# Dense feed-forward up products: the activations' high and low parts side by side in one 512-column product

## The reference

```
def swiglu(x, w13, w2):                      # block 1, layer 0
    a, g = jnp.split(x @ w13, 2, axis=-1)
    return (jax.nn.silu(a) * g) @ w2

# block 2, each layer
h = rms_norm(x, norm_ffn_g[l])
u = causal_depthwise_conv(h @ ffn_w_up[l], ffn_conv_w[l], ffn_conv_b[l])   # width 3
x = x + (jax.nn.silu(u[..., :D_FF]) * u[..., D_FF:]) @ ffn_w_down[l]
```

## Time and profile before

| what | us |
|---|---|
| median of 3 runs (lowest, highest) | 2723.18 (2722.4, 2725.64) |
| the profiled execution, first to last instruction | 2724.5 |
| TensorE busy in it | 2412.8 (89%) |
| VectorE busy | 1805.8 (66%) |
| ScalarE busy | 1325.7 (49%) |
| GpSimd busy | 251.4 (9%) |

### The profile page before, as it was taken

The page is one execution under the profiler, slowest core; times in us unless marked ns, Lnnn a source line. Parts: engine busy times, 40 slices in busy tenths (PEclk is TensorE's granted clock), DMA queues, the critical chain, the costliest instruction groups (busy, mean ns, idle before and its releaser), DMA issues.

```text
span 2724.5 us, 42692 instructions
## 1 busy us (share of the span) xinstructions
PE 2412.8 (89%) x16461; PEld 2211.7 (81%) x16461; DVE 1805.8 (66%) x1724; ACT 1325.7 (49%) x1183; POOL 251.4 (9%) x208
## 2 busy tenths in 40 slices
PE   7879799777859999999999999997877998977998
PEld 7768799777859797979797979796766998866997
DVE  4454544546448687878787878787663677763776
ACT  3433333343327576767676767674342444332443
POOL 1300000130000000000000000000660000750000
PEclk9889899888969999999999999999877999967999
DMA  9224455522429798989898989897322455312451
GB/s 291 78 86 147 139 185 185 157 78 93 152 68 366 271 364 275 364 281 365 279 367 279 362 283 367 278 367 256 120 76 70 145 183 181 122 62 70 155 185 62
DMA packets 429765, 559.49 MB, mean 205 GB/s; under 512 B 9598, under 2 KB 384868, under 8 KB 429424
## 3 DMA queue, kind: packets, MB, share of 16 engines
q1 hardware_dynamic: 425376, 545.05, 59.2%
q0 software_dynamic: 4304, 13.25, 1.7%
HBM read 557.20 MB, written 1.06 MB: 205 GB/s over the span
## 4 chain that ended last, share of the span: by engine, by line
issue 44%; PE 39%; POOL 5%; DVE 5%; POOLq 3%; ACT 2%; DVEq 1%; DMA 1%; SPq 0%; ACTq 0%
PE ps L567 11%; PE ps L568 11%; PE ps L569 11%; POOL st L548 2%; POOLq L547 2%; POOL st L542 2%; POOL ht L491 1%; PE ps L600 1%; PE ps L1074 1%; PE ps L778 1%; PE ps L1054 1%; POOLq L495 1%; PE ps L752 0%; DVE xn L1505 0%; DVE w_lo L1443 0%
## 5 line engine op out<-in xcount | busy, mean ns | idle before, releaser
L1443 DVE TENSOR_TENSOR w_lo<-raw,w_hi 128x2048 fp32r<-128x2048 f32 x519 | 1191.3, 2302 | 448.9 <-ACT w_hi L1131 446.3
L1131 ACT ACTIVATE w_hi<-raw 128x2048 fp32r<-128x2048 f32 x519 | 985.4, 1908 | 245.1 <-PE ps L569 234.5
L567 PE MATMUL ps<-w_hi,xg_hi 128*128 128x256 f32 x1792 | 511.9, 286 | 16.3 <-DVE w_lo L1443 16.1
L568 PE MATMUL ps<-w_lo,xg_hi 128*128 128x256 f32 x1792 | 500.7, 279 | 0.0
L569 PE MATMUL ps<-w_hi,xg_lo 128*128 128x256 f32 x1792 | 500.7, 279 | 0.0
L567 PE MATMUL ps<-xT_hi,w_hi 128*128 128x256 f32 x1504 | 436.3, 290 | 22.7 <-DVE xT_lo L1458 15.0
L568 PE MATMUL ps<-xT_lo,w_hi 128*128 128x256 f32 x1504 | 433.1, 288 | 0.0
L569 PE MATMUL ps<-xT_hi,w_lo 128*128 128x256 f32 x1504 | 432.9, 288 | 0.0
L567 PEld LDWEIGHTS ps<-w_hi,xg_hi 128*128 128x128 f32 x1792 | 337.8, 188 | 26.7 <-DVE w_lo L1443 19.6
L568 PEld LDWEIGHTS ps<-w_lo,xg_hi 128*128 128x128 f32 x1792 | 341.5, 191 | 3.6
L569 PEld LDWEIGHTS ps<-w_hi,xg_lo 128*128 128x128 f32 x1792 | 337.9, 189 | 0.0
(11 more groups left out here) (458 smaller groups left out, 3150.0 us busy)
## 6 DMA issues: line engine op xcount, KB each, us to landing
raw<-in_exp_w SPq DMA_DIRECT2D x336, 1024.0 KB, 7.5
raw<-in_ffn_w_up SPq DMA_DIRECT2D x44, 1024.0 KB, 5.1
raw<-in_w_in SPq DMA_DIRECT2D x42, 1024.0 KB, 5.9
raw<-in_ffn_w SPq DMA_DIRECT2D x33, 1024.0 KB, 5.1
raw<-in_ffn_w_down SPq DMA_DIRECT2D x22, 1024.0 KB, 5.4
raw<-in_w_gate SPq DMA_DIRECT2D x16, 1024.0 KB, 5.3
raw<-in_w_out SPq DMA_DIRECT2D x8, 1024.0 KB, 5.0
raw<-in_w_o SPq DMA_DIRECT2D x6, 1024.0 KB, 5.0
```

Source lines behind the costliest of these rows:

```text
L567: pe.matmul(out, lhs[0], rhs[0], start=first, stop=False)
L568: pe.matmul(out, lhs[0], rhs[1], start=False, stop=False)
L1131: act.activation(w_hi[:, u.const % SPL, 0:width], raw[:, u.const % RAW, 0:width], ACT.Copy)\
L1443: dve.tensor_tensor(w_lo[:, u.const % SPL, 0:width], raw[:, u.const % RAW, 0:width], w_hi[:, u.const % SPL, 0:width].bitcast(F32), ALU.sub ...
```

## The change

`xT_hi` and `xT_lo` become two views of one tile `xT` in which, for each of the 8 chunks, the 256 columns of the high part lie beside the 256 of the low part. In the dense feed-forwards' up product the high weight block multiplies all 512 columns in one matmul, and the low weight block the 256 of the high part, into the first half of the same bank. The two halves of a bank are added afterwards: ScalarE copies the first halves out of PSUM, VectorE adds the second halves to the copy (`add_half`, one instruction of 2 x 256 elements and a drain). An up unit now needs two banks: A uses 4 and 5, G uses 6 and 7, in every step, and TensorE waits for the additions of the step before (`up_in`). In block 1 Silu is taken after the addition, from `sa` to `sa`, and `hf` first receives G. The counters of the two kinds of feed-forward become one set, so the counts of block 2 begin at DENSE_STEPS.

```diff
--- before.py
+++ after.py
@@ -197,8 +197,8 @@
         w_hi = sb("w_hi", [P, SPL, UW], F32R)
         w_lo = sb("w_lo", [P, SPL, UW], F32R)
         x = sb("x", [P, TT, D])
-        xT_hi = sb("xT_hi", [P, KC, S], F32R)
-        xT_lo = sb("xT_lo", [P, KC, S], F32R)
+        xT = sb("xT", [P, KC, 2, S], F32R)
+        xT_hi, xT_lo = xT[:, :, 0, :], xT[:, :, 1, :]
         yA_hi = sb("yA_hi", [P, 4, S], F32R)
         yA_lo = sb("yA_lo", [P, 4, S], F32R)
         with ExitStack() as shared:
@@ -340,8 +340,9 @@
         raw_landed = [ctx.enter_context(nc.semaphore(f"raw_landed{i}")) for i in range(RAW)]
         block = ctx.enter_context(nc.Block())
         yb, qgT, kgT, kdT, sTm = vb, qcT, laT, cumT, dm
-        F1 = {"h": hf, "h_ready": S_.h1_ready, "h_hi_ready": S_.h1_hi_ready, "h_lo_ready": S_.h1_lo_ready}
-        F2 = {"h": h2f, "h_ready": S_.h2_ready, "h_hi_ready": S_.h2_hi_ready, "h_lo_ready": S_.h2_lo_ready}
+        FF = {"half_ready": S_.half_ready, "up_in": S_.up_in, "h_ready": S_.h_ready, "h_hi_ready": S_.h_hi_ready,
+              "h_lo_ready": S_.h_lo_ready}
+        F1, F2 = {"h": hf, **FF}, {"h": h2f, **FF}
 
         def bank(b, *shape):
 
@@ -614,13 +615,22 @@
             def feed_forward(u, steps, count, hh, hl, sig):
 
                 def up(at, b):
-                    project_T(at, b)
+
+                    w = unit_parts(at, KC, FFC)
+                    for c in range(2):
+                        o = ps[:, b + c, :]
+                        for k in range(KC):
+                            hi, lo = [v[:, k, c * P:(c + 1) * P] for v in w]
+                            pe.matmul(o, hi, xT[:, k, :, :].rearrange("p a n -> p (a n)"), start=k == 0, stop=False)
+                            m = pe.matmul(o[:, 0:S], lo, xT_hi[:, k, :], start=False, stop=k == KC - 1)
+                    m.then_inc(S_.unit_used, 1)
 
                 def step_up(j, at, odd, dyn):
 
-                    pe.wait_ge(sig["h_ready"], dyn.value(plus=1))
-                    up(at, 4 + 2 * odd)
-                    up(at + 1, 5 + 2 * odd)
+                    pe.wait_ge(sig["up_in"], dyn.value(2, 1))
+                    up(at, 4)
+                    pe.wait_ge(sig["up_in"], dyn.value(2, 2))
+                    up(at + 1, 6)
 
                 def down(at, odd, dyn):
 
@@ -1118,7 +1128,7 @@
             with pe.Fori(0, 2) as L:
                 u = block2_units(passes).loop(L, LAYER2_UNITS)
                 mixer2(L, u)
-                feed_forward(u + MIX2_UNITS, DENSE_STEPS, Count(0).loop(L, DENSE_STEPS), h2_hi, h2_lo, F2)
+                feed_forward(u + MIX2_UNITS, DENSE_STEPS, Count(DENSE_STEPS).loop(L, DENSE_STEPS), h2_hi, h2_lo, F2)
                 close_sums()
 
 
@@ -1177,20 +1187,23 @@
 
             def silu1(at, odd, dyn, after):
 
-                act.wait_ge(S_.h1_ready, dyn.value(plus=1))
                 used(at)
-                act.activation(sa[:, odd], ps[:, 4 + 2 * odd, :], ACT.Silu).then_inc(S_.silu1_ready, 1)
+                act.activation(sa[:, odd].rearrange("p (c n) -> p c n", c=2), ps[:, 4:6, 0:S], ACT.Copy).then_inc(S_.half_ready, 1)
                 split(after)
+                act.wait_ge(S_.up_in, dyn.value(2, 3))
+                act.activation(sa[:, odd], sa[:, odd], ACT.Silu).then_inc(S_.silu1_ready, 1)
+                used(at + 1)
+                act.activation(hf[:, odd].rearrange("p (c n) -> p c n", c=2), ps[:, 6:8, 0:S], ACT.Copy).then_inc(S_.half_ready, 1)
 
             def conv2(at, odd, dyn, after):
 
-                act.wait_ge(S_.h2_ready, dyn.value(plus=1))
+                act.wait_ge(S_.h_ready, dyn.value(plus=1))
                 used(at)
-                act.activation(u_a[:, odd, :, 2:], bank(4 + 2 * odd, 2, S), ACT.Copy).then_inc(S_.ua_ready, 1)
+                act.activation(u_a[:, odd, :, 2:], ps[:, 4:6, 0:S], ACT.Copy).then_inc(S_.half_ready, 1)
                 split(after)
                 used(at + 1)
-                act.activation(u_g[:, odd, :, 2:], bank(5 + 2 * odd, 2, S), ACT.Copy).then_inc(S_.ug_ready, 1)
-                act.wait_ge(S_.ca_ready, dyn.value(plus=1))
+                act.activation(u_g[:, odd, :, 2:], ps[:, 6:8, 0:S], ACT.Copy).then_inc(S_.half_ready, 1)
+                act.wait_ge(S_.ca_ready, dyn.value(plus=1 - DENSE_STEPS))
                 act.activation(c_a[:, odd], c_a[:, odd], ACT.Silu).then_inc(S_.silu2_ready, 1)
 
             def mixer1(L, u):
@@ -1427,7 +1440,7 @@
                 u = block2_units(passes).loop(L, LAYER2_UNITS)
                 mixer2(L, u)
                 at = u + MIX2_UNITS
-                feed_forward(at, DENSE_STEPS, Count(0).loop(L, DENSE_STEPS), h2_hi, F2, conv2)
+                feed_forward(at, DENSE_STEPS, Count(DENSE_STEPS).loop(L, DENSE_STEPS), h2_hi, F2, conv2)
                 with act.If(L == 0):
                     split_next(at + STEP * DENSE_STEPS)
                 with act.Else():
@@ -1532,11 +1545,19 @@
                 for j in range(2 * pairs + 1, steps):
                     step(u + (2 + STEP * (j - 1)), j % 2, count + j, False)
 
+            def add_half(v, b):
+
+                dve.tensor_tensor(v, v, ps[:, b:b + 2, S:2 * S], ALU.add).then_inc(S_.up_in, 1)
+                dve.drain()
+
             def dense_hidden(at, odd, dyn, after):
+                dve.wait_ge(S_.half_ready, dyn.value(2, 1))
+                add_half(sa[:, odd].rearrange("p (c n) -> p c n", c=2), 4)
+                split(after)
+                dve.wait_ge(S_.half_ready, dyn.value(2, 2))
+                add_half(hf[:, odd].rearrange("p (c n) -> p c n", c=2), 6)
                 dve.wait_ge(S_.silu1_ready, dyn.value(plus=1))
-                split(after)
-                used(at + 1)
-                dve.tensor_tensor(hf[:, odd], sa[:, odd], ps[:, 5 + 2 * odd, :], ALU.mult).then_inc(S_.h1_ready, 1)
+                dve.tensor_tensor(hf[:, odd], sa[:, odd], hf[:, odd], ALU.mult).then_inc(S_.h_ready, 1)
 
             def less_max(sc, mx):
                 dve.reduce_max(mx, sc, AX_X)
@@ -2016,7 +2037,7 @@
             def conv_ffn(L):
                 def hidden(at, odd, dyn, after):
 
-                    j = Count(dyn.const, dyn.terms[1:]).value() * 2
+                    j = Count(dyn.const - DENSE_STEPS, dyn.terms[1:]).value() * 2
 
                     def columns(src, dst, first):
                         for k in range(3):
@@ -2032,20 +2053,22 @@
                                 dve.drain()
                         return m
 
-                    dve.wait_ge(S_.ua_ready, dyn.value(plus=1))
+                    dve.wait_ge(S_.half_ready, dyn.value(2, 1))
+                    add_half(u_a[:, odd, :, 2:], 4)
                     columns(u_a, c_a[:, odd], 0).then_inc(S_.ca_ready, 1)
                     split(after)
-                    dve.wait_ge(S_.ug_ready, dyn.value(plus=1))
+                    dve.wait_ge(S_.half_ready, dyn.value(2, 2))
+                    add_half(u_g[:, odd, :, 2:], 6)
                     columns(u_g, c_g, 22)
                     dve.drain()
-                    dve.wait_ge(S_.silu2_ready, dyn.value(plus=1))
+                    dve.wait_ge(S_.silu2_ready, dyn.value(plus=1 - DENSE_STEPS))
                     dve.tensor_tensor(h2f[:, odd].rearrange("p (c n) -> p c n", c=2), c_a[:, odd], c_g[:], ALU.mult)\
-                       .then_inc(S_.h2_ready, 1)
+                       .then_inc(S_.h_ready, 1)
                 return hidden
 
             dve.memset(zeros[:], 0.0)
-            dve.memset(stat[:, 1:2], 0.0).then_inc(S_.h1_ready, 2)
-            dve.memset(stat[:, 2:3], 0.0).then_inc(S_.h2_ready, 2)
+            dve.memset(stat[:, 1:2], 0.0).then_inc(S_.h_ready, 2)
+            dve.memset(stat[:, 2:3], 0.0).then_inc(S_.up_in, 2)
             dve.memset(stat[:, 3:4], 0.0).then_inc(S_.lo_ready, RAW)
             dve.memset(stat[:, 4:5], 0.0).then_inc(S_.xn_ready, 1)
             for n in range(AHEAD):
@@ -2068,7 +2091,7 @@
                 u = block2_units(passes).loop(L, LAYER2_UNITS)
                 mixer2(L, u)
                 at = u + MIX2_UNITS
-                feed_forward(at, DENSE_STEPS, Count(0).loop(L, DENSE_STEPS), h2_hi, h2_lo, F2, conv_ffn(L))
+                feed_forward(at, DENSE_STEPS, Count(DENSE_STEPS).loop(L, DENSE_STEPS), h2_hi, h2_lo, F2, conv_ffn(L))
                 with dve.If(L == 0):
                     split_next(at + STEP * DENSE_STEPS)
                 with dve.Else():
```

## The result

| kernel | median us (runs) | ratio to before, 95% interval |
|---|---|---|
| before | 2725.64 (7) | |
| changed | 2735.69 (7) | 1.0038 (1.0025 to 1.0051) |
| changed, run again later | 2736.14 (10), before 2726.93 (15) | 1.0035 (1.0022 to 1.0048) |

The changed kernel is 10 us slower. I had forecast 5.6 us slower, 2728.8, and a range up to 2734, so sign and place were right and the size was not. Part of the distance in absolute time isn't the change's: the median of the kernel before is 2725.64 over seven runs, where three had given 2723.18. The profiled execution of the changed kernel has a span of 2733.9 us, against 2724.5. The ratios of this document leave out two executions that took several times as long as all others, one of the kernel before (10206 us) and one of `best` (7705 us), and the medians count them.

The account below looks back on a forecast made before the run. TensorE was taken to bound both dense feed-forwards, with VectorE taking over block 2's step after the change. Block 1's -3.8 and block 2's +9.4 gave +5.6 us on the median 2723.18, so 2728.8 us, range 2724.5 to 2734.

Parts of the forecast that it names:

- TensorE in block 2: Block 2's dense feed-forwards: TensorE's own step falls from 17.10 to 16.70 us, as up units need fewer matmuls.
- VectorE's loop in block 2: Block 2's steps: 15.55 us without waits plus 1.91 for additions and lags gives 17.46, so VectorE sets the step, +0.36.
- PSUM banks and hand-shakes: Block 2's up units: giving up the second pair of PSUM banks costs nothing; additions free banks long before TensorE returns.
- Start of block 2: First steps of block 2's feed-forwards: G(1) begins 0.8 us later at the lower clock, c_g(1) is 1.4 late.
- End of block 2: Last down product, D(10), of block 2's feed-forwards: all lateness reaches the end, +4.7 us a layer, +9.4 for two.
- my high end: Upper forecast: block 1 saves 2.0 and loses 2.7 to the clock, block 2 +5.2 a layer; together +11, 2734 us.
- the loop that I closed on paper: Block 2's step timed from addition A at 0: nothing of TensorE's is late; it waits 0.7 us for G's weights.
- Block 1: Block 1's feed-forward: TensorE stays the bound; 19 up units save 0.20 each, 3.8 us (lower bound 2.0); start zero.
- (1): All three feed-forward stages: TensorE bounds them if additions cost VectorE under 1.15 us a step; 2713 us; chance 0.07.
- (2): Block 2's steps: TensorE's new small waits let its clock fall, some 20 falls cost 40 us; 2769; chance 0.06.
- (3): Block 2's steps: lag at the lower bound, 17.27 a step, little moves: +1.8, 2725; low end of forecast, no own chance.
- (4): Up product: halves don't run as one matmul, no 512-column rows on xT, TensorE slower; chance 0.02.

Follow-up runs that it names:

- best: Changed kernel plus block 2's first tap A on ScalarE, block 1's 512-column matmuls grouped first, 128-row fillers in block 2: 2715.87 us, 0.9951 of before.
- small_add: Changed kernel, but each block 2 addition covers only 2 of 256 columns of each bank: 2717.68 us, 0.9975 of before.
- tap_on_act: Changed kernel, but block 2's first tap over A runs on ScalarE instead of VectorE: 2721.13 us, 0.9985 of before.
- tap_order: tap_on_act, but each half of an up unit does its 8 matmuls of 512 columns before the 8 of 256: 2725.1 us (one run).
- double_add: Changed kernel with every addition done twice, the first into a spare tile, in both blocks: 2776.2 us (one run).
- tap_pad: tap_on_act with 24 bytes a partition left free ahead of block 2's tiles, aligning u, c and h to 1024 bytes: 2720.0 us (one run).
- before_fill: Kernel before with 14 matmuls of zeros between G(0) and A(1) of block 2's feed-forwards: 2724.24 us, 0.9996 of before.
- after_fill: Changed kernel with 32-row zero matmuls in block 2, 14 between G(0) and A(1), 12 before the last down product: 2736.06 us, 1.0033 of before.
- tap_on_act_fill: tap_on_act plus block 2 fillers, 14 between G(0) and A(1) and 5 before the last down product: 2715.89 us, 0.9966 of before.
- after_fill128: after_fill, but fillers have all 128 rows and move real xT against stationary zeros, 512 columns each: 2737.8 us (one run).

## Why the prediction was right and wrong

- **TensorE in block 2: right.** Its own step was forecast at 16.70 and measured 16.70 once VectorE was relieved (small_add, tap_on_act).
- **VectorE's loop in block 2: right.** Forecast 17.46, measured 17.50 and 17.55 in turn. Additions 0.68; the lags behind them 0.34 and 0.24 (forecast 0.31 and 0.22). The h2f product begins 0.16 to 0.20 behind the taps where it was 0.07, which I didn't have; its cause isn't shown.
- **PSUM banks and hand-shakes cost nothing: right** (small_add keeps them).
- **Start of block 2: right in kind, and lucky in the sum.** G(1) began 0.6 and 0.7 later (forecast 0.8; my own terms, 1.00 + 0.91 - 0.91 - 0.08, add up to 0.9). That it would run at the lower clock was right for one layer of two. So c_g(1) came 0.1 and 1.2 late instead of 1.4, and nine steps brought 3.9 instead of 3.2, as each grew by 0.43 and not by 0.36. D(10) began 4.1 and 5.2 late, forecast 4.7. That the two together are 9.3 against 9.4 is luck: the clock that layer 1 kept made up for the longer steps.
- **End of block 2: the step that failed.** "At the end D(10) waits for h_lo already today (0.4), so all of it reaches the end: +4.7 a layer". I carried the lateness through but didn't ask how long TensorE itself stands idle there. It runs ahead of VectorE, so its wait grew from 0.4 to 2.7 us, and behind it the clock fell: +1.5 us a layer, 3.0 in all. With it block 2 lost 5.6 and 6.7 us a layer, more than the 5.2 of my high end. Waits of 1.46 us (tap_on_act) at the same place left D(10) at 5.8. I had priced this fall for the small waits in the steps, where it didn't come, and for block 1's start, not for the one long wait that my own numbers gave. In the loop that I closed on paper TensorE ends G at 3.4 and D at 9.0. VectorE begins addition G at 5.96 and is done with h's low part 0.91 + 2.91 + 1.40 + 0.69 later, at 11.9. That is an estimated wait of 2.9 for D(10), and it was 2.7.
- **Block 1: the term was mis-sized.** "the 19 up units after the start save 19 x 0.20 = 3.8 us (2.0 at the lower bound)". A pair costs 0.353, not 0.3475, so a unit saves 0.11, the lower bound, and as the down product takes 5.50 instead of 5.46 the step saves 0.18 instead of 0.40: about 1.7. The start cost 0.4 more, where I had put nothing; its wait of 1.44 left the clock up. I took the 0.2275 of block 1's down matmuls, which are a row of one kind; in alternation with 256 columns block 1 doesn't reach it (tap_order does).
- **Rivals.** (1) didn't occur: VectorE's additions cost more than its slack, but with short additions its condition holds and the step is the 16.70 that it names. (2) didn't occur: waits of 0.4 to 0.6 once a step left the clock at 1.00. Its mechanism exists at longer waits (four falls behind twelve waits of 1.65 to 1.78 in double_add). Its price was wrong there: a fall in a step that VectorE sets cost nothing. (3) and (4) are excluded by the steps and the 512-column rows on xT.

By stages: forecast -3.8 + 9.4 = +5.6; the profile -1.3 + 12.3 = +11.0 there, of which 9.3 lateness and 3.0 clock in block 2, and -1.6 elsewhere. Against the median before of its own series the kernel lost 10.0 us, within the +11 of my high end; in absolute time it lies over 2734 because that median rose by 2.5.

## What to carry to other kernels

A gain on the busiest engine is worth at most the distance to the next loop: write down the second engine's whole loop without its waits, with everything the change gives it, before pricing the first. Where that engine takes over, the first one runs ahead of it, and its longest waits stand at the start and the end of the stage (here 3.3 and 2.7 us, against 0.4 to 0.6 in a step); price them with the clock, not only the lateness. And once the binding engine is known, moving a small piece of any of its work (here one tap of two instructions to an idle ScalarE) can turn the loss into a gain, of 0.15% by itself and up to 0.5% with the rest. A gain in one stage is sure only when the stages behind it are looked at too.

## What the runs showed of the hardware that I had not expected

- The lower clock behind a wait is not a matter of the wait's length alone. In one profile of the changed kernel TensorE went on at 2.4 GHz after 3.26 us of idling and at 1.2 after 3.06 in the next layer; in another of the same kernel it fell after 3.25 and not after 3.06. After 2.73 to 2.75 us before D(10) it fell all eight times, after 1.65 to 1.78 in double_add four times of twelve, after 1.46 or less at D(10) never (tap_on_act, tap_order and tap_pad, both layers).
- In place of the wait before D(10), fillers over 32 rows of zeros left it at 5.8 us in one layer and at 7.35 in the other; fillers over 128 rows with real moving data left it at 5.8 in both (one run). At G(1) fillers over 32 rows kept the clock at 2.4 GHz all six times (before_fill, after_fill, tap_on_act_fill).
- A stage that gets shorter can be followed by one that gets longer with the same code: behind the filled stage of before_fill, after_fill and after_fill128 the mixer took 2.3 to 5.4 us more than without fillers, at a mean clock of 0.77 to 0.78 instead of 0.79. In `best` it didn't (187.1 us, tap_on_act 188.0).
- The distance between matmuls of one shape isn't fixed by shape and operands: the same pairs of 512 and 256 columns ran at 0.353 us in block 1 and 0.347 in block 2, and grouping by size took block 1 to 0.226 for 512 columns and made block 2 slightly slower.
- An instruction with addresses computed at run time starts 0.34 (c_a) or 0.24 us (c_g) behind a drained 0.68 us one; why the two differ isn't shown. Without the drain it starts 0.08 before the end of the one ahead.
